# Moving activation tiles by 32 bytes in SBUF, in a two-block fp32 kernel bound by TensorE

## The reference

```python
# first block: mLSTM mixer, MLP, short-convolution mixer, MLP; post-norms
h = rms_norm(x, g[0]); h = mixer(h); x = x + rms_norm(h, g[1])
h = relu(rms_norm(x, g[2]) @ w_up); x = x + rms_norm((h * h) @ w_down, g[3])   # 1024 -> 4096 -> 1024, twice
# second block: retention and pooling, cross attention to 256 memory rows, gated MLP with a convolution
x = x + concat([y_ret, y_pool]) @ w_out
x = x + cross_attn(rmsnorm(x), mem_n, wq, wkv, wo)
x = x + (silu(gate) * val) @ w_down                                            # 1024 -> 2 x 2816 -> 1024
return rmsnorm(x, final_norm_g)
```

## Time and profile before

| | |
|---|---|
| median of three runs | 994.25 us (993.46 to 1000.04) |
| the profiled execution, its own time | 992.6 us |
| its span, first to last instruction | 990.5 us |
| instructions | 20138 |
| PE busy | 961.8 us, 97% |
| PEld busy | 950.9 us, 96% |
| DVE busy | 648.3 us, 65% |
| ACT busy | 537.0 us, 54% |
| POOL busy | 144.2 us, 15% |
| mean granted TensorE clock | 0.993 |

### The profile page before, as it was taken

How to read it: one execution, slowest core, us unless ns; L and a number is a source line. 1 busy time by engine, 2 the same in 40 slices (tenths; PEclk the granted TensorE clock), 3 DMA queues, 4 the chain that set the end, 5 groups by cost and what they waited for, 6 DMA issues and landing times.

```text
span 990.5 us, 20138 instructions
## 1 busy us (share of the span) xinstructions
PE 961.8 (97%) x8062; PEld 950.9 (96%) x8062; DVE 648.3 (65%) x839; ACT 537.0 (54%) x754; POOL 144.2 (15%) x129
## 2 busy tenths in 40 slices
PE   8999989999999899989999999899999999999996
PEld 8999989999999899989999999899999999999995
DVE  6567576665444877587655444894775779999642
ACT  5566656654443555556555444565554557666541
POOL 2121140000010400159000000414120110000001
PEclk9999999999999999999999999999999999999998
DMA  9533636555545355545455553663433545555521
GB/s 337 198 128 111 217 123 207 194 197 191 207 169 202 109 203 191 190 134 207 170 195 188 179 203 113 217 210 130 163 136 127 171 144 197 201 180 177 206 86 43
DMA packets 25844, 172.17 MB, mean 174 GB/s; under 512 B 3252, under 2 KB 3892, under 8 KB 5432
## 3 DMA queue, kind: packets, MB, share of 16 engines
q1 hardware_dynamic: 25784, 171.30, 49.7%
HBM read 170.24 MB, written 1.05 MB: 173 GB/s over the span
## 4 chain that ended last, share of the span: by engine, by line
PE 80%; DVE 7%; issue 1%; POOL 1%; ACT 1%; DVEq 0%; ACTq 0%; POOLq 0%
PE po L403 25%; PE po L404 24%; PE po L405 24%; DVE xnL L1241 3%; DVE wL L1234 2%; PE po L431 1%; PE po L432 1%; PE po L430 1%; POOL rtok L1810 1%; PE pc L732 1%; PE pn L471 1%; PE pn L481 1%; DVE y L1441 0%; PE pn L710 0%; PE pa L710 0%
## 5 line engine op out<-in xcount | busy, mean ns | idle before, releaser
L794 ACT ACTIVATE wH<-raw 128x1024 fp32r<-128x1024 f32 x318 | 335.4, 1059 | 297.9 <-PE po L405 267.5
L1234 DVE TENSOR_TENSOR wL<-raw,wH 128x1024 fp32r<-128x1024 f32 x318 | 387.8, 1244 | 157.0 <-ACT wH L794 156.6
L403 PE MATMUL po<-xnH,wH 128*128 128x256 f32 x1376 | 392.2, 285 | 15.2 <-DVE xnL L1241 12.4
L404 PE MATMUL po<-xnL,wH 128*128 128x256 f32 x1376 | 385.1, 280 | 0.0
L405 PE MATMUL po<-xnH,wL 128*128 128x256 f32 x1376 | 385.1, 280 | 0.0
L403 PEld LDWEIGHTS po<-xnH,wH 128*128 128x128 f32 x1376 | 262.3, 191 | 19.3 <-DVE xnL L1241 10.3
L404 PEld LDWEIGHTS po<-xnL,wH 128*128 128x128 f32 x1376 | 260.4, 189 | 0.2
L405 PEld LDWEIGHTS po<-xnH,wL 128*128 128x128 f32 x1376 | 260.0, 189 | 0.0
L403 PE MATMUL po<-hH,wH 128*128 128x256 f32 x688 | 192.0, 279 | 0.0
L404 PE MATMUL po<-hL,wH 128*128 128x256 f32 x688 | 192.0, 279 | 0.0
L405 PE MATMUL po<-hH,wL 128*128 128x256 f32 x688 | 192.0, 279 | 0.0
(11 more groups left out here) (283 smaller groups left out, 1052.7 us busy)
## 6 DMA issues: line engine op xcount, KB each, us to landing
raw<-in_weights SPq DMA_DIRECT2D x158, 1024.0 KB, 4.8
x<-in_xT SPq DMA_DIRECT2D x4, 256.0 KB, 6.4
raw<-in_weights SPq DMA_DIRECT2D x2, 512.0 KB, 6.3
mem<-in_memT SPq DMA_DIRECT2D x1, 1024.0 KB, 12.7
out<-y SPq DMA_DIRECT2D x4, 256.0 KB, 2.4
decayt<-in_decay SPq DMA_DIRECT2D x1, 512.0 KB, 3.7
poolwt<-in_poolw SPq DMA_DIRECT2D x1, 256.0 KB, 3.7
par<-in_params SPq DMA_DIRECT2D x1, 164.0 KB, 3.4
```

The costliest lines, as they stand in the source:

```text
L403: pe.matmul(psum[:, n, 0:T], wH[w][:, wc], aH[:, ac, :], start=start, stop=False)
L404: pe.matmul(psum[:, n, 0:T], wH[w][:, wc], aL[:, ac, :], start=False, stop=False)
L794: act.activation(wH[b % HL][:, hs], raw[b % RAW][:, hs], ACT.Copy).then_inc(s_hi, 1)
L1234: dve.tensor_tensor(wL[b % HL][:, hs], raw[b % RAW][:, hs], wH[b % HL][:, hs].bitcast(f32), ALU.subtract)\
```

## The change

Two edits, both to addresses. The tile warm is allocated behind xnL and no longer ahead of ms, and scratch begins 32 bytes behind the end of spare. No instruction, wait, shape or order differs.

```diff
         par = sb("par", [P, NPAR], f32)
-        warm = sb("warm", [P, 1], f32)
         ms = sb("ms", [P, TT], f32)
         minus_half = sb("minus_half", [P, 2 * NH], f32)
         rtok = sb("rtok", [P, TT], f32)
         rmem = sb("rmem", [P, TT], f32)
         xnH = sb("xnH", [P, C, T], f32r)
         xnL = sb("xnL", [P, C, T], f32r)
+        warm = sb("warm", [P, 1], f32)
         memH = sb("memH", [P, C, T], f32r)
...
         spare = sb("spare", [P, TT, P], f32)
-        scratch = place[0]
+        scratch = place[0] + 32
         at = [scratch]
         y = sb("y", [P, C, T], f32, at)
```

## The result

The changed kernel takes 1007.57 us (median of 7 runs, 1006.82 to 1009.53) against 995.19 us (7 runs, 992.65 to 1000.42) before: ratio 1.0117, 95% interval [1.0089, 1.0145]. It is slower by 1.2%, and the spread of its runs is 2.7 us where the kernel before spreads over 7.8. The profiled execution took 1007.51 us with a span of 1005.5; the comparable one before took 992.6 with 990.5. The prediction was 993 in 974 to 1007 and failed; the slow rival had been worked out at 1008. In every ratio of this document runs that lie over 1.5% above the fastest of their own kernel are left out, some of the kernel before among them, so a ratio is not the quotient of the medians beside it.

A forecast was written before the change was run, and what follows sets the result against it. The prediction took TensorE's matmul pace (busy 97% of the span) to bound the kernel. Its three steps each came to zero, leaving the profiled 992.6 us + 0, forecast as 993 us, range 974 to 1007.

The forecast's parts named there:

- the slow rival: Main matmul stream: the shift makes the slow pace the rule, 4.5 ns per matmul, 1008 us if all slow; chance 0.21.
- The bound, and the two paces: TensorE's matmul stream bounds the kernel, at a fast or slow pace 4.5 ns apart at identical addresses.
- Step 1: Main matmuls, 7248 of 7632 with changed distance to the weights: zero change, between −19 us all fast and +15 all slow.
- the upper bound given, +15: Main matmuls if every one goes slow: (1911 + 1425) × 4.5 ns = +15 us.
- Steps 2 and 3: VectorE and ScalarE work: zero, within ±0.6 us; DMAs whose targets move: zero, 0.05 us on the last store.
- only two paces: Assumption for TensorE's matmul stream that just two paces exist, 113.2 and 117.6 ns; any other would break the forecast.
- an even split: Some 2850 main matmuls outside the counted stretches, taken as about 1425 fast and 1425 slow.
- The test named for it: Count of matmuls in the same long stretches of the changed kernel: 1414 in 160 us is fast, 1360 slow.
- the fast rival: Main matmul stream: the shift parts weight load and streamed read; 974 us if all goes fast; chance 0.29.
- my forecast: Whole kernel: the change only redraws the hiccups that pick the pace, 6 us either way, 993 us; chance 0.50.
- The remark on the role of the tiles: In slabs by token, with activation loaded and weight streaming, both paces appear, so pace does not depend on tile roles.
- The page's rule: TensorE has two SBUF read ports and never waits; 16-byte cachelines make a 32-byte shift alike, so zero change.

The follow-up runs named there:

- e3: Whole layout, weight tiles included, placed 32 bytes higher than in the kernel before, all distances between tiles kept: 991.34 us, ratio 1.0017.
- s4: Against the kernel before, par and small tiles moved behind xnL; xn at 352, mem, mix and h at 288 above the weights modulo 512: 1010.60 us, ratio 1.0170.
- e4: All activation tiles of the kernel before moved by 64 bytes, to 0 modulo 512 above the weights: 1018.70 us, ratio 1.0329.
- v1: Against the kernel before, chunk 0 of xnH and xnL put at distance 0, the other seven at 192 modulo 256: 982.36 us, ratio 0.9898.
- s2: Against the kernel before, par and small tiles moved behind xnL; xn at 256, mem, mix and h at 192 above the weights: 1002.12 us, ratio 1.0097.

## Why the prediction was wrong

**The bound, and the two paces: right.** TensorE's matmul stream carried the whole difference, the clock did not move (0.993 before, 0.994 after), and one long stretch that falls into the slow pace costs what was worked out: 6.4 us, against 6.6 in the MLP of layer 0.

**Step 1 failed.** It put the cost of the moved distances at zero "because identical addresses show both paces and the offset seen shows neither gain nor loss". The first half is true and does not carry the conclusion. Two paces at distance 448 say that this distance allows two states; they say nothing of the others, and none of the other seven shows 113 ns in a long stretch. The second half compared the wrong quantity: prob was taken for its start modulo 64, and e3 shows that a start at 32 modulo 64 costs nothing if the weights move along. The measured value of the term is +15.0 us in the span, and the upper bound given, +15, was its size. That bound has a slip of its own: the 2850 matmuls split evenly include the 384 on mem tiles, which kept their distance.

**Steps 2 and 3 were right**: VectorE's and ScalarE's groups stayed within 1%, and the output's stores still take 2.4 us to land.

**The slow rival was right in kind and near in time**, 1008 us against 1007.57, with the shift making a slow pace the rule. In detail the "only two paces" did not hold: the moved tiles run at 117.3 to 118.7 ns, not at 117.7. That the sum met the measurement to 0.4 us is in part luck. It gave 8.6 us to the stretches that had been fast (1911 × 4.5 ns) and 6.4 to an even split that no row supports, and nothing to stretches that were slow already; measured are 6.6 and 1.5 us in the blocks of the fast stretches, and of the other 6.9 us some lies in stretches slow before (1.2 in the MLP of layer 1). The test named for it (1360 matmuls in 160 us) came out to the matmul, with neither of the two paces in it at the value assumed (117.5 and 118.3). The reason against the fast rival and for my forecast was the same argument, and it weighed too much at 0.50.

**The remark on the role of the tiles held for the two paces and hid the distance.** By token, the streamed weight lies at −448, which is 64 modulo 256, and both paces were seen there. With the activation streaming at 64 the same two were seen, 117.8 in all long stretches and 113.4 on mem. But a role turned round is another distance unless it is 0 or 128, as the 120 and 117.3 ns of s4 show, so the rows of the kernel before held two distances, and not one as the prediction took them.

**The page's rule.** The Trainium skill, "SBUF — State Buffer", section "Who interferes with whom", has TensorE never waiting on anyone at its two read ports, and by it the change would cost nothing. The trace does not agree: with nothing but the distance of the two operands changed, a pair of weight load and matmul takes from 113.4 to 120 ns, and e4 takes 3.3% longer than the kernel before. Here the measurement decides.

**Still open.** Why the period is 256 bytes, and what in the reads meets, is not shown. That both streams read SBUF in step and collide by their distance fits every run, and no run looked inside. Nor is it shown what in a hiccup draws the lock; v1 shows only that with six matmuls at distance 0 in each slab every long stretch of xn and the h behind it came out fast, and s2 and v1 have mix stretches that came out slow all the same.

## What to carry to other kernels

Where a stream of weight loads and f32r matmuls bounds a kernel, take its pace from counts in stretches without a gap, per tile, and treat the distance between loaded and streamed operand as a tuning parameter: here 32 bytes cost 1.2%, 64 bytes 3.3%. Moving small tiles about does that unseen, so a change that only allocates can move the time. Runs that differ by a fixed amount (6.6 us here, one stretch's worth) can be a sign of a lock between two states, and such a lock can be steered.

## What the runs showed of the hardware that was not expected

- The pace of a 128 x 128 load with a 128 x 256 f32r matmul at full granted clock depends on the distance of the operands modulo 256 bytes, from 113.4 ns (192) to 120 ns (0), and on its sign (352 streaming 120, 352 loaded 117.3); an absolute shift of both by 32 bytes changes nothing (ratio 1.0017 [0.9966, 1.0068]).
- At one distance (192 modulo 256) the stream can lock into either of two paces and keep it for over 1400 matmuls.
- Six matmuls at distance 0 ahead of 42 at 192 gave the fast lock in every long stretch of xn and h in the one profiled execution of v1; two did not do so reliably. The runs of v1 spread over 2.3 us (4 runs), those with two over 10.5 (12 runs).
